# A hybrid decoder layer with expert retrieval: the last mix tile's product in the next phase, y in four parts, two PSUM pairs for the tile sums, 54 candidates

## The chip, the cores and the metric

One core of a Trainium2 chip runs the whole program. The metric is the device time of one execution in microseconds; the kernel before has a median of 3254.82 us over three timed runs (3250.97 to 3257.0). Engines are named as in the profile: TensorE (PE), VectorE (DVE), ScalarE (ACT), GpSimd (POOL) and SyncE (SP), and SP and POOL issue the transfers.

## The reference, cut to what matters

One layer over 1024 prompt rows and 64 sample rows of width 1024, all in float32. Attention and a diagonal state-space mixer work on the same projected input; their outputs are normalised, projected by `w_out` and added to x. Then each row retrieves experts:

```
proj = rmsnorm(x) @ w_in + b_in                      # q, k, v and u
attn = window_attention(q, k, v)                     # window 128, sinks
y    = gelu(Re(C h) + D u);  y = y * sigmoid(y @ w_glu + b_glu)
x    = x + concat(rmsnorm(attn), rmsnorm(y)) @ w_out
xn   = rmsnorm(x)
s    = (xn @ w_query) . keys                         # per head: 2 x 128 scores
top_s, top_i = top_k(s, 16)                          # of either half
best = top_k(top_s[0][:, None] + top_s[1][None, :], 16)   # of 256 pairs
act  = gelu(u_table[idx] . xn)                       # 8 heads x 16 experts
x    = rmsnorm(x + sum(softmax(best) * act * v_table[idx]))
```

Only a pair (a, b) of ranks with (a+1)(b+1) <= 16 can be among the best 16 of the sums, which is why both kernels form far fewer than 256 candidates per head.

## The kernel before, in words

The program has three phases, each a block with a barrier at its end.

**Mix** (`mix_tokens`) walks over eight tiles of 128 prompt rows. In step t it projects tile t+1, computes the attention of tile t and finishes tile t-1: `take_attention` puts the weighted values, scaled, into aT; `mix` multiplies aT by the upper half of `w_out` (w_top) into PJ; `sum_squares` sums sq over the partitions; `mean_square`, `rstd_a` and `add_residual` (L449) make x1 in xk, and `store_x1` writes it to scratch. For the last tile these follow the last step, and the phase ends when SP has seen its stores land. VectorE also makes two matrices for the next phase, in `input_matrices` (L632 to L638): the real one in the last step, the imaginary one after it.

**State-space mixer and sample rows** (`run_ssm_and_samples`). The scan runs on VectorE; TensorE makes the sample attention beside it. At its end TensorE makes the outputs y in four parts (Y_ORDER, four column groups), ScalarE and VectorE copy each from PSUM into U2 and SP stores it as y_ssm. Tile 0's y goes straight to `early.y` by one transfer (L989), issued behind the fourth part.

**Retrieval** (`retrieve_experts`) walks over eight prompt tiles and one of samples. A prompt tile has 128 slots (NSLOT): in each, POOL issues an indirect gather of one row of the joint u and v table per partition, 1 MB, into a ring of eight (L1515). VectorE multiplies the u half by xn and sums it (`product`, L1884). For each pair of slots ScalarE applies GELU (L1637), weighs (L1650) and makes two diagonal matrices (L1657), and TensorE adds the v half times the diagonal into ACC (`add_v`, L2086). Slot s may be gathered again when TensorE is done with it (semaphore pv).

While tile t is gathered, tile t+1 is prepared. `prepared` gives for each slot which step (h, j) of which tile runs there: in steady tiles (t+1, h+1, j) in slot 16h+j, and in the last 16 slots (t+2, 0, j). The steps of row 0 work on y: GELU at (0, 3), turning at (0, 4), its product with w_glu into ZS at (0, 9) (L1969), its sum at (0, 13), sigmoid at (0, 14) (L1574). Row 2 makes the product with the lower half of `w_out` into OP (L1983) and the residual sum xr; rows 3 and 4 the scores (L2008), rows 4 and 5 the best 16 of each half, row 6 the candidates and the best 16 of them, and from (6, 14) on VectorE finds the number of each chosen expert by a subtraction and a reduction over 16 x NCAND columns (L1805, L1806). The candidates share a buffer with yT, their numbers one with z.

Slot 121 (SPREAD) spreads the next tile's rows over two groups: `spread_rows` writes them into OP and TQ (L2065), and `take_rows` copies them to xn (L1631). When a tile ends, VectorE does products 0 and 1 of the next, then `sum_out`: it waits for the last addition, copies ACC (L1890) and sums the squares; `begin` (L2076) on TensorE waits for that copy and opens ACC again with the residual. POOL's `root` stands behind gather 11 (L1542), `norm_out` on VectorE (L1900) behind product 6.

PSUM has eight banks: ACC, TQ, ZS and OP have two each.

## Time and profile before

| what | us |
|---|---|
| median of three runs | 3254.82 (3250.97 to 3257.0) |
| the profiled execution | 3267.73, its span 3265.8 |
| TensorE busy | 2296.5 (70%) |
| VectorE busy | 2172.5 (67%) |
| POOL busy | 1347.3 (41%) |
| ScalarE busy | 931.3 (29%) |
| first gather issued | 442.49 |
| gathers (1088 of them), share of the 16 DMA engines' span | 85.5% |

The profile is of one execution and its times are those of that execution. Its chain of the work that ended last gives 32% of the span to the gathers, 22% to TensorE, 17% to VectorE. The windows used below give for a stretch the busy time of each engine, the mean granted clock of TensorE (1.00 is 2.4 GHz, 0.50 is 1.2 GHz), the share of time in which the DMA engines had packets, and the rate at which they moved them. Many products here run through a line that all tiles share, so a line's mean hides the stage; the stretches don't.

### The profile page before, as it was taken

How to read it: one execution, taken by the hardware profiler on the slowest of the kernel's cores; microseconds unless marked ns; L12 is line 12 of the kernel's file. 1: busy time of each engine (PE TensorE's matmuls, PEld its weight loads, DVE VectorE, ACT ScalarE, POOL GpSimd, SP SyncE). 2: the span in 40 equal slices, each digit the busy share in tenths (PEclk: the TensorE clock that was granted, in tenths of full speed). 3: DMA queues.
4: the chain of work that ended last, by engine and by line, in shares of the span. 5: the costliest groups of instructions: out<-in, count | busy, mean ns of one | idle time of the engine just before them, and what ended most of it. 6: DMA issues, size and time to landing. Idle time of an engine off the chain costs nothing.

```text
span 3265.8 us, 28428 instructions
## 1 busy us (share of the span) xinstructions
PE 2296.5 (70%) x7579; PEld 784.0 (24%) x7579; DVE 2172.5 (67%) x5144; ACT 931.3 (29%) x3193; POOL 1347.3 (41%) x1265
## 2 busy tenths in 40 slices
PE   8998777776685658566856685668566856676576
PEld 4555543311121112111211121112111211121121
DVE  4545568788568656865686568656865686568644
ACT  2222234323222322232223222322232223222222
POOL 1232024444444454444444544444444444444442
PEclk9998898877787788777877887778777878896899
DMA  5223489999999999999999999999999999999998
GB/s 196 79 75 93 119 340 396 365 399 367 421 421 408 416 411 421 406 414 404 421 415 411 420 422 407 408 420 421 409 421 405 421 412 421 404 421 417 421 414 337
DMA packets 187553, 1208.00 MB, mean 370 GB/s; under 512 B 26552, under 2 KB 33768, under 8 KB 46928
## 3 DMA queue, kind: packets, MB, share of 16 engines
q0 software_dynamic: 157344, 1142.99, 85.5%
q1 hardware_dynamic: 30048, 63.20, 5.5%
q8 instruction: 60, 0.98, 0.1%
q14 instruction: 101, 0.83, 0.1%
HBM read 1190.30 MB, written 15.42 MB: 369 GB/s over the span
## 4 chain that ended last, share of the span: by engine, by line
DMA 32%; PE 22%; DVE 17%; issue 7%; ACT 5%; POOL 4%; DVEq 0%; POOLq 0%; ACTq 0%
DMA uv_ring<-in_uv_table,idx 32%; PE ACC L2086 14%; DVE uv_ring L1884 9%; PE ZS L2008 5%; POOL uv_ring L1515 4%; ACT dg L1657 2%; PE OP L1983 1%; ACT dot L1650 1%; DVE idx_f L1806 1%; DVE S L1805 1%; ACT dot L1637 1%; DVE pos L1730 1%; DVE pos L1727 1%; DVE best L1729 0%; DVE yT_and_cand L1728 0%
## 5 line engine op out<-in xcount | busy, mean ns | idle before, releaser
L2086 PE MATMUL ACC<-uv_ring,dg 128*64 128x512 f32 x4352 | 1466.3, 785 | 895.9 <-ACT dg L1657 895.7
L1515 POOL DMA_INDIRECT uv_ring<-in_uv_table,idx x1088 | 1254.5, 1153 | 1546.7 <-PE ACC L2086 1321.6
L1884 DVE CUSTOM_DVE_ANT_0 uv_ring<-uv_ring,xn 128x1024 f32<-128x1024 f32 x1088 | 1325.6, 1226 | 706.1 <-DMA uv_ring<-in_uv_table,idx 667.0
L2086 PEld LDWEIGHTS ACC<-uv_ring,dg 128*64 128x64 f32 x4352 | 341.1, 165 | 1951.0 <-ACT dg L1657 1381.8
L1637 ACT ACTIVATE dot<-dot 128x2 f32<-128x2 f32 x544 | 110.6, 203 | 1886.2 <-DVE dot L1884 1885.9
L1657 ACT ACTIVATE dg<-stack,dot 128x64 f32<-128x64 f32 x1088 | 324.1, 340 | 17.7
L1650 ACT ACTIVATE dot<-gate,dot 128x1 f32<-128x1 f32 x1088 | 261.2, 287 | 18.9
L2008 PE MATMUL ZS<-score_w,xnT 128*128 128x512 f32 x512 | 242.4, 614 | 0.0
L527 PE MATMUL PJ<-w_in,xT 128*128 128x512 f32 (+1 forms) x384 | 143.8, 532 | 3.2 <-DVE pj L407 3.2
L2008 PEld LDWEIGHTS ZS<-score_w,xnT 128*128 128x128 f32 x512 | 93.4, 194 | 158.9 <-issue 158.9
L1884 DVE DVE_READ_ACCUMULATOR2_ANT dot<- 128x1 f32 x1088 | 89.5, 82 | 0.0
L527 PEld LDWEIGHTS PJ<-w_in,xT 128*128 128x128 f32 x384 | 72.8, 193 | 68.7 <-issue 65.8
L1806 DVE TENSOR_REDUCE idx_f<-S 128x16 f32<-128x992 f32 x64 | 75.9, 1186 | 2.2
L1805 DVE TENSOR_TENSOR S<-z_and_cid,pos_f 128x992 f32<-128x992 f32 x64 | 76.1, 1189 | 0.0
L1983 PE MATMUL OP<-w_bot,yT_and_cand 128*128 128x512 f32 x144 | 66.1, 603 | 0.8 <-issue 0.8
L1726 DVE MAX8 top_v<-S 128x8 f32<-128x128 f32 x144 | 41.8, 290 | 25.6 <-ACT S L1589 18.0
L375 ACT ACTIVATE pr<-pr,small_a 128x256 f32<-128x256 f32 x64 | 31.6, 494 | 93.8 <-DVE small_a L470 93.8
L561 PE MATMUL PJ<-w_top,aT 128*128 128x512 f32 x128 | 56.8, 597 | 1.8 <-issue 0.8
L1729 DVE MAX8 top_v<-S 128x8 f32<-128x128 f32 x144 | 42.5, 295 | 15.2 <-DVE S L1728 0.5
L294 POOL TENSOR_SCALAR stat_a<-stat_a 128x1 f32<-128x1 f32 x9 | 1.8, 205 | 104.6 <-ACT xt L360 81.3
L1542 POOL TENSOR_TENSOR stat_e<-stat_e,minus_half 128x1 f32<-128x1 f32 x27 | 17.3, 649 | 66.3 <-DVE stat_e L1761 33.1
L1727 DVE FIND_INDEX8 top_i<-top_v,S 128x8 uint32<-128x128 f32 x144 | 41.1, 285 | 0.6 <-issue 0.6
(337 smaller groups left out, 1598.1 us busy)
## 6 DMA issues: line engine op xcount, KB each, us to landing
uv_ring<-in_uv_table,idx POOLq DMA_INDIRECT x1088, 10.9
score_w<-in_w_query SPq DMA_DIRECT2D x8, 1024.0 KB, 19.2
w_in<-in_w_in SPq DMA_DIRECT2D x8, 640.0 KB, 9.2
xt<-in_x SPq DMA_DIRECT2D x9, 512.0 KB, 4.7
xr<-scratch_x SPq DMA_DIRECT2D x9, 512.0 KB, 8.3
xc<-in_x_columns SPq DMA_DIRECT2D x8, 512.0 KB, 3.9
xk<-in_x SPq DMA_DIRECT2D x8, 512.0 KB, 3.8
scratch_x<-xk SPq DMA_DIRECT2D x8, 512.0 KB, 2.6
```

The costliest lines, as they stand in the source:

```text
L527: ins = nc.tensor.matmul(PJ[:, b, 0:hi - lo], xT[:, j, :], w_in[:, j, lo:hi], start=(j == 0), stop=(j == KD - 1))
L1515: pool.indirect_dma_start(out=ring[:, s_ % RING, :], out_offset=None, in_=a["uv_table"], in_offset=bass.IndirectOffsetOnAxis(ap=idx[:, s_: ...
L1637: A(act_w[:, cols], dot[:, cols], ACT.Gelu).then_inc(gelus, 1)
L1650: ins = A(wgt[:, n:n + 1], gate[:, n:n + 1], ACT.Copy, scale=act_w[:, n:n + 1])
L1657: A(dg[:, s_ % DG, :], stack[:], ACT.Copy, scale=wgt[:, s_:s_ + 1]).then_inc(diags, 1)
L1727: V.max_index(where[:, 0:8], vals[:, 0:8], src)
L1805: dch_(V.tensor_tensor(match, bcast(cid[:, e, :], KS, 1), bcast(pos_f[:, e, :], NCAND, 2), ALU.subtract))
L1806: dch_(V.tensor_reduce(idx_f[:, e, :], match, AX.X, ALU.min, apply_absolute_value=True))
L1884: V.tensor_tensor_reduce(row, row, xn[:, g, :], 1.0, 0.0, ALU.mult, ALU.add, dot[:, s_:s_ + 1]).then_inc(dots, 1)
L1983: ins = nc.tensor.matmul(OP[:, b, :], yT[:, n, :], w_bot[:, n, 512 * b:512 * b + 512], start=(n == 0), stop=(n == SW // P - 1))
L2008: ins = nc.tensor.matmul(ZS[:, bank, :], xnT[:, m, :], score_w[:, c_:c_ + 4, m, :], start=(m == 0), stop=(m == KD - 1))
L2086: ins = nc.tensor.matmul(ACC[GT * g:GT * (g + 1), b, :], dg[:, n % DG, :], ring[:, n % RING, D + 512 * b:D + 512 * b + 512], start=False, ...
```

## The change

1. **Mix.** The last tile's product, its sum of squares and its residual leave the mix phase. aT, sq and the odd x buffer move to `shared`; the next phase's TensorE does the sum of squares and the product right after it has turned the cached keys, into banks 5 to 7; ScalarE copies the sum and, scaled by the root that POOL makes, the product over sq and aT; VectorE adds it to x between the first and the second part of y, and SP stores it behind the second. TensorE's sample outputs wait for ScalarE's copy, since they use the same banks. `input_matrices` moves: the real half ahead of `mean_square` in the last step, the imaginary half into the real one's place.
2. **y.** Each of its four parts is carried to `early.y` by itself, and ScalarE applies GELU to a constant at the end of the second phase.
3. **PSUM.** OP goes; ACC becomes a pair of pairs, used in turns by the tiles. The spreading and the product with `w_out` go into ZS (for the first tile and the second into the pair that is still free). `begin` of the next tile follows `spread_rows`. `sum_out` comes behind product 4 of the next tile, the root behind gather 13, `norm_out` behind product 8. The steps (t+2, 0, j) begin at slot 100 (106 in the first tile) instead of 112.
4. **Candidates.** The blocks of ranks form 54 instead of 62 candidates per head.

The first excerpt is TensorE's order in the second phase: the turning of the cached keys (kc), and what follows it. U2g and XT are the operands of the sample outputs, qT_s the turned queries.

```order
L1244 MATMUL PA<-ident,kc 128x128 x8
L1274 MATMUL PA<-T,qT_s 32x136 x16
L1252 MATMUL PA<-U2g,XT 8x128 x8
L1259 MATMUL PA<-WC_r,H_and_WBt 8x128 x2
L1259 MATMUL PA<-WC_i,H_and_WBt 8x128 x2
```

The same place of the changed kernel:

```order
L1261 MATMUL PA<-ident,kc 128x128 x8
L1266 MATMUL PA<-one_s,sq_and_aT 128x1 x4
L1271 MATMUL PA<-w_top,sq_and_aT 128x512 x8
L1302 MATMUL PA<-T,qT_s 32x136 x16
L1280 MATMUL PA<-U2g,XT 8x128 x8
L1287 MATMUL PA<-WC_r,H_and_WBt 8x128 x2
```

The last mix tile's sum of squares and product now stand between the keys and the scores; they stood at the end of the first phase.

The second excerpt is TensorE's order where one steady tile passes to the next, before the change. The first row is the end of a long run of additions of tile t (four rows to a pair of slots).

```order
L2086 MATMUL ACC<-uv_ring,dg 64x512 x8
L1969 MATMUL ZS<-early,yT_and_cand 128x512 x4
L2065 MATMUL OP<-xn_next,spread 128x512 x2
L2065 MATMUL TQ<-xn_next,spread 128x512 x2
L2086 MATMUL ACC<-uv_ring,dg 64x512 x12
L2076 MATMUL ACC<-xr,ident 128x512 x2
L2086 MATMUL ACC<-uv_ring,dg 64x512 x24
```

And in the changed kernel, where the names of both pairs are printed as ACC:

```order
L1998 MATMUL TQ<-ident,early 128x128 x4
L2128 MATMUL ACC<-uv_ring,dg 64x512 x8
L2009 MATMUL ZS<-early,yT_and_cand 128x512 x4
L2128 MATMUL ACC<-uv_ring,dg 64x512 x24
L2105 MATMUL ZS<-xn_next,spread 128x512 x2
L2105 MATMUL TQ<-xn_next,spread 128x512 x2
L2118 MATMUL ACC<-xr,ident 128x512 x2
L2128 MATMUL ACC<-uv_ring,dg 64x512 x36
```

The residual stood after the tile's last addition and stands now three pairs ahead of it, right behind the spreading; y's product moved away from the spreading by six pairs.

The third is VectorE's order at the same change of tile, before: four products (the last two of tile t, the first two of t+1), then the copy of the sum.

```order
L1756 TENSOR_TENSOR z_and_cid<-ZS,early 128x512
...
L1884 ISA uv_ring,dot<-uv_ring,xn 128x1024
L1884 ISA dot 128x1
L1890 COPY S<-ACC 128x1024
L1892 ISA xn_next,stat_e<-S 128x1024
L1892 ISA stat_e 128x1
L1895 TENSOR_SCALAR stat_e<-stat_e 128x1
L1884 ISA uv_ring,dot<-uv_ring,xn 128x1024
```

In the changed kernel:

```order
L1799 ISA z_and_cid,stat_e<-early 128x512
L1799 ISA stat_e 128x1
L1800 TENSOR_SCALAR stat_e<-stat_e 128x1
L1924 ISA uv_ring,dot<-uv_ring,xn 128x1024
L1924 ISA dot 128x1
L1930 COPY S<-ACC 128x1024
L1932 ISA xn_next,stat_e<-S 128x1024
L1932 ISA stat_e 128x1
```

The copy came before product 2 and comes now behind product 4, and y's own square sum (step (1, 3)) stands ahead of it.

```diff
@@ mix_tokens, VectorE
                         scale_columns(t + 1, 1 - p)
-
+                        if last:
+                            par.input_matrices(nc, dve, 0)
                         mean_square(t - 1)
...
                     if last:
-                        par.input_matrices(nc, dve, 0)
+                        par.input_matrices(nc, dve, 1)
...
                 take_attention(PT - 1)
-                par.input_matrices(nc, dve, 1)
-                mean_square(PT - 1)
-                add_residual(PT - 1, 1)
@@ mix_tokens, TensorE
-                mix(PT - 1)
-                sum_squares(PT - 1)
@@ run_ssm_and_samples, SP
-                    if n == 3:
-                        early.y_in.mark(sp.dma_start(early.y, U2[0:P // L, :].rearrange("c (j n) -> c j n", j=L)))
+                    if n == 2:
+                        sp.wait_ge(ev["x1_7"], 1)
+                        sp.dma_start(s["x1"][bass.ts(PT - 1, P), :], x1_7[:]).then_inc(stores, 16)
                     cols = slice(i * SW // 4, (i + 1) * SW // 4)
+                    sp.dma_start(early.y[:, cols], U2[0:P // L, :].rearrange("c (j n) -> c j n", j=L)[:, :, cols]
+                                 ).then_inc(early.first_y_in, 16)
@@ POOL
+                pool.wait_ge(ev["summed_7"], 1)
+                pool.tensor_scalar(ms_7, ss_7, 1.0 / AW, EPS, ALU.mult, ALU.add).then_inc(ev["ms_7"], 1)
+                pool.wait_ge(ev["ms_7"], 1)
+                pool.tensor_tensor(rstd_7, ms_7, half[:], ALU.pow).then_inc(ev["rstd_7"], 1)
@@ ScalarE
+                act.wait_ge(ev["squares_7"], 1)
+                A(ss_7, XS_7, ACT.Copy).then_inc(ev["summed_7"], 1)
+                act.wait_ge(ev["mixed_7"], 1)
+                act.wait_ge(ev["rstd_7"], 1)
+                A(attention_7, MO_7.rearrange("p b n -> p (b n)"), ACT.Copy, scale=rstd_7).then_inc(ev["scaled_7"], 1)
...
+                act.wait_ge(ev["one"], 1)
+                A(small[:, 7, 0:1], one[:], ACT.Gelu)
@@ VectorE
                 for n, i in enumerate(Y_ORDER):
+                    if n == 1:
+                        dve.wait_ge(ev["scaled_7"], 1)
+                        shared.xk_in.of(dve, PT - 1)
+                        tt(x1_7[:], x1_7[:], attention_7, ALU.add).then_inc(ev["x1_7"], 1)
                     take_outputs(n, i)
@@ TensorE
+                shared.sq_done.of(pe, PT - 1)
+                for r in range(REP):
+                    ins = nc.tensor.matmul(XS_7, shared.sq[:, r, :], one[:], start=(r == 0), stop=(r == REP - 1))
+                ins.then_inc(ev["squares_7"], 1)
+                shared.aT_done.of(pe, PT - 1)
+                for b in range(2):
+                    for r in range(REP):
+                        ins = nc.tensor.matmul(MO_7[:, b, :], shared.aT[:, r, :], w_top[:, r, 512 * b:512 * b + 512],
+                                               start=(r == 0), stop=(r == REP - 1))
+                ins.then_inc(ev["mixed_7"], 1)
...
+                pe.wait_ge(ev["scaled_7"], 1)
                 for i in range(3):
                     sample_outputs(i)
@@ retrieve_experts
-        OUT_AT = LEAD + 3
-        BLOCKS = ((0, 2, 16), (2, 4, 5), (4, 8, 3), (8, 16, 1))
+        SUM_AT, OUT_AT = LEAD + 1, LEAD + 5
+        EARLY_Y = {"first": 106, "steady": 100}
+        BLOCKS = ((0, 1, 16), (1, 2, 8), (2, 4, 5), (4, 8, 3), (8, 16, 1))
...
-                return own + ([(2, 0, j)] if h == EH - 1 else [])
-            if h < EH - 1:
-                return [(t + 1, h + 1, j)]
-            return [(t + 2, 0, j)] if turn == "steady" else []
+            else:
+                own = [(t + 1, h + 1, j)] if h < EH - 1 else []
+            y_step = s_ - EARLY_Y[turn] if turn in EARLY_Y else -1
+            return own + ([(t + 2, 0, y_step)] if 0 <= y_step < KS else [])
+        def spread_bank(t, g):
+            return TQ if g else ACCS[1] if t == 0 else ZS
+        def product_bank(t):
+            return ACCS[1] if t == 1 else ZS
@@ VectorE, retrieve
                         product(t, s_)
+                        if s_ == SUM_AT and turn != "first":
+                            sum_out(t - 1, P, t * NSLOT)
...
-                        for s_ in range(LEAD - 1):
+                        for s_ in range(LEAD):
                             product(t + 1, s_)
-                        sum_out(t, P, t * NSLOT + slots_of(turn))
-                        product(t + 1, LEAD - 1)
@@ TensorE, begin and retrieve
-                    k["acc_taken"].of(pe, t - 1)
+                    k["acc_taken"].of(pe, t - 2)
...
-                    begin(t)
...
                                     k["yT_done"].of(pe, t + 2)
+                                    k["zb_done"].of(pe, t + 2)
+                                k["S_b"].of(pe, t + 1)
                                 for g in range(GROUPS):
                                     spread_rows(t + 1, g)
+                                begin(t + 1)
```

## Rows read from the trace of the kernel before

**Rows 1.** Windows of busy time: us of each engine, clock, DMA share, GB/s.

```profile
core 0: us, PE busy (x) PEld busy (x) DVE busy (x) ACT busy (x) POOL busy (x), PEclk, DMA share, GB/s
450.00:3240.00 2790.00, 1884.72 (x5462) 535.09 (x5463) 1930.91 (x4538) 814.72 (x2884) 1264.32 (x1106) 0.81 1.00 411
450.00:770.00 320.00, 229.41 (x772) 83.72 (x772) 259.14 (x784) 114.57 (x350) 135.57 (x116) 0.81 0.97 387
1175.00:1325.00 150.00, 110.36 (x328) 32.81 (x328) 97.67 (x238) 41.12 (x156) 68.29 (x61) 0.86 1.01 421
775.00:805.00 30.00, 20.76 (x68) 6.56 (x66) 18.71 (x39) 12.63 (x36) 13.57 (x12) 0.84 0.97 376
...
3095.00:3125.00 30.00, 25.17 (x50) 7.19 (x47) 17.42 (x28) 7.62 (x30) 13.99 (x12) 0.83 0.99 398
1030.00:1060.00 30.00, 19.37 (x52) 3.96 (x48) 26.17 (x53) 10.49 (x33) 13.18 (x12) 0.66 0.98 388
...
2990.00:3020.00 30.00, 17.42 (x52) 3.75 (x48) 25.55 (x64) 10.49 (x33) 12.86 (x12) 0.67 1.01 409
```

**Rows 2.** Timeline, end of the mix phase: start, us, engine, line, operation [idle before].

```profile
258.49 0.16 DVE L435 TENSOR_SCALAR stat_a<-X 128x1 f32<-128x1 f32 x1 [5.04 <-PE X L552]
...
269.05 2.19 DVE L440 TENSOR_SCALAR pr<-pr,small_a 128x256 f32<-128x256 f32 x8
271.16 2.29 DVE L632 TENSOR_TENSOR T<-PR_r,BB_r 128x2048 f32<-128x2048 f32 x1
...
274.17 1.91 PE L594 MATMUL SC<-ident,pr 128*128 128x128 f32 x16
...
282.49 0.54 SPq L280 DMA_DIRECT2D scratch_pj<-pj  x1
...
283.21 7.11 PE L561 MATMUL PJ<-w_top,aT 128*128 128x512 f32 x16 [0.83 <-issue]
...
293.69 0.33 SPq L230 DMA_DIRECT2D scratch_x<-xk  x1
296.65 0.33 SPq L957 DMA_DIRECT2D U<-scratch_u  x1
```

**Rows 3.** Timeline of the second phase: TensorE's hole, and a part of y.

```profile
340.44 1.19 PE L1274 MATMUL PA<-T,qT_s 64*32 64x136 f32 x32 [6.66 <-DVE T L1109]
...
341.56 2.94 PE L1252 MATMUL PA<-U2g,XT 128*8 128x128 f32 x16
...
347.51 1.91 PE L1252 MATMUL PA<-U2g,XT 128*8 128x128 f32 x16 [1.16 <-ACT U L1040]
...
383.52 0.69 DVE L1182 COPY U<-PA 128x512 f32<-128x512 f32 x1 [3.20 <-PE PA L1259]
```

**Rows 4.** Timeline of ScalarE at the start of the third phase.

```profile
396.07 1.28 ACT L1568 ACT_TABLE_LOAD   x1 [4.02 <-PEq L2143]
397.36 0.63 ACT L1568 ACTIVATE early<-early 128x512 f32<-128x512 f32 x1
```

**Rows 5.** Timelines of ScalarE, TensorE and VectorE where tile 1 passes to tile 2.

```profile
1130.39 1.28 ACT L1637 ACT_TABLE_LOAD   x1
1130.43 3.68 PE L2086 MATMUL ACC<-uv_ring,dg 128*64 128x512 f32 x8 [5.04 <-ACT dg L1657]
1134.25 1.22 DVE L1890 COPY S<-ACC 128x1024 f32<-128x1024 f32 x1 [2.97 <-PE ACC L2086]
1135.62 3.63 PE L2076 MATMUL ACC<-xr,ident 128*128 128x512 f32 x4 [1.51 <-DVE S L1890]
1148.21 1.28 DVE L1900 SCALAR_TENSOR_TENSOR S<-S,stat_e,g_fin 128x1024 f32<-128x1024 f32 x1 [4.04 <-POOL stat_e L1542]
```

**Rows 6.** TensorE's timeline at slot 121, and the gathers of 1112 to 1166.

```profile
1114.67 3.70 PE L1969 MATMUL ZS<-early,yT_and_cand 128*128 128x512 f32 x8
1118.21 1.88 PE L2065 MATMUL OP<-xn_next,spread 128*128 128x512 f32 x4
...
DMA to landing us min/median/max: 6.7/11.0/15.2
```

**Rows 7.** Groups by form: busy us, mean ns of one, idle before.

```profile
L1805 DVE TENSOR_TENSOR S<-z_and_cid,pos_f 128x992 f32<-128x992 f32 x64 | 76.1, 1189 | 0.0
```

71 lines of the change are left out of this document (40 added, 31 removed).

## The prediction, made before the changed kernel ran

> **What bounds the kernel now.** I read the windows first. From 450 to 3240 us the DMA engines have a busy share of 1.00 [rows 1]: the eight prompt tiles and the sample tile are fetched there, 1088 gathers of 1 MB each. The last column says how far this stage is from its own ceiling. A quiet stretch runs at 421 GB/s, the whole stage at 411 [rows 1]. Against a ceiling of 421.5 the stage loses 2790 x 10.5 / 421.5 = 69.5 us. Nothing can be won there but these microseconds. Where they lie: I took eight stretches of 30 us, each where one tile passes to the next (the first and the last of them are shown); by the same formula they lose 3.2, 3.3, 4.5, 2.4, 2.5, 3.5, 3.6 and 1.7 us, 24.7 in all. Seven stretches, one per tile, in which VectorE chooses the next tile's experts lose 14.1 (2.4 in the first shown, 0.9 in the last). The first tile, 450 to 770, loses 26.2 [rows 1]. That is 65 of the 69.5.
>
> Before 450 us the DMA engines mostly wait, and the time is a chain through the engines: each microsecond taken out of that chain comes off the end, as all gathers come sooner.
>
> The profiled execution took 3267.7 us, 1.9 more than its span, and lies 12.9 above the median of the three timed runs, 3254.8. The sum is made against 3267.7 and then taken off the median; the 0.4% between them changes a saving of 40 us by 0.2.
>
> **Part 1, the end of the mix phase.** Now the last tile's product (16 records, 7.11 us), its sum of squares, the root and the residual stand at the end, and only half of input_matrices runs beside them; the store's issue begins at 293.69 and ends at 294.02, and the next phase starts at 296.65, 2.63 later [rows 2]. Afterwards the last thing that phase waits for is the copy to scratch_pj, issued at 282.49 + 0.54 = 283.03. But one thing gets later first: the first half of input_matrices, three operations of 2.29, 6.8 us from 271.16 with the waits between them, moves ahead of mean_square, into a hole of 5.04 us that ends at 258.49 [rows 2]. It overfills it by about 1.9 us (it can start at 253.4, after scale_columns, and ends at 260.3 instead of 258.5). The second half takes the first's old place, so VectorE stays 1.9 late to the end. TensorE does not: its transposes at 274.17 wait for probabilities that are ready at 269.05 + 2.19 = 271.2 and would be at 273.1 [rows 2]. So the phase ends at 283.03 + 1.9 + 2.63 = 287.6, **-9.1 us**. If the landing of the stores takes a microsecond more or less, -8 to -10.
>
> **Part 2, the product in the next phase.** TensorE has a hole of 6.66 us from 333.78, while VectorE multiplies, until kT is there at 340.44 [rows 3]. The inserted work is 0.95 + 7.11 = 8.1 us at the full clock, so the scores start about 1.4 late, and the sample outputs wait for ScalarE's copy of the product out of PSUM (VectorE takes 1.22 for as many columns [rows 5]) and start at about 343.1 instead of 341.56. Against this, TensorE no longer idles: today the first batch of L1252 after the hole takes 2.94 us, the next 1.91 [rows 3]; with the hole filled I take 1.91 for the first too. Net **+0.5**. The bounds: -0.6 if VectorE's own chain hides it, +1.6 if the batch stays slow, +8 if the product itself ran at the lower clock. What TensorE did before the hole speaks against the last: it was busy without a pause, and the first batch only got slow behind the 6.66 idle. POOL's two small operations on the root lie ahead of the product's end; VectorE's addition of 1024 columns (1.2 us, as its other 1024-column operations) is put between two parts of y, where VectorE waits 3.2 us for each [rows 3], so it is hidden, and so is the store of x1, which goes out two parts before the phase's last store.
>
> **Part 3, y in four parts and the early GELU.** Today y's transfer is issued whole at the end, the next phase starts, ScalarE loads its table for 1.28 us and the GELU starts at 397.36, right behind it [rows 4]. With the table loaded before the phase's end and only a quarter of y left to carry, it can start at 396.1: **-1.3** (0 if the y transfer is what lands last, -2 at best). Here the Trainium skill (ScalarE: Activation LUTs, What ACT_TABLE_LOAD costs) counts a drain of about 1.4 us behind each load, 2.66 in all. The row has the GELU 10 ns behind the load's end, so the drain isn't seen; by the page this term would be -2.7. Fewer candidates on the way to the first gather: -0.1.
>
> **Part 4, the change of tile.** This is the largest term. At the change the chain is: ScalarE loads the sigmoid's table and then GELU's again, the second at 1130.39, between the last two diagonals; the last pair of products starts at 1130.43 at the lower clock (3.68); VectorE, which has stopped for it, copies the sum at 1134.25; only then the residual enters the same PSUM pair at 1135.62 (3.63), and the new tile's first products run at 1139.18. Then VectorE stops again, 4.04 us up to 1148.21, for a root that stands in POOL's queue behind a gather which itself waits for TensorE [rows 5]. Afterwards the new tile has its own pair, its residual is added at step 121 of 128, the sigmoid comes 12 steps earlier (six at the first change), and VectorE takes the sum after product 4, when TensorE has long been done. No wait of this chain is left but the root's: gather 13 must be issued before it, and VectorE wants it after product 8. The order of the two is as now (gather 11, product 6), but nothing has stalled before, so I give it 0 to 2 us, within what the ring hides. I take 85% of 24.7: **-21**. Bounds 0 (the loss stays) and -24.7.
>
> What moves to another place: y's projection (3.70) and the spreading (two halves of 1.88) stood back to back at step 121 at the full clock, 7.4 us [rows 6], and the rate fell only later, at the change itself. Now the projection stands at step 109, and at 121 spreading and residual, 3.8 + 1.9 to 3.6 = 5.7 to 7.4. That is what the ring swallowed before. At the lower clock it would be 7.5 + 3.6 = 11.1, and the projection 7.4.
>
> **Part 5, 54 candidates.** Each of the 64 subtractions and 64 reductions over 992 columns takes 1.19 us [rows 7]; at 864 columns at most 0.15 less each, about 2.2 us of VectorE per tile, and 0.3 on the best-16 searches; one more small operation in each pairwise table gives back about 0.2. In steps 96 to 108 VectorE is full, so the ring refills faster, but the loss of 14.1 begins in the searches before, where only the 0.3 helps. I take **-5** (0 to -14). In the first tile the same pieces shrink: **-3** (0 to -8) of its 26.2; the rest there is TensorE's making of weights, which is not touched.
>
> **The sum.** -9.1 + 0.5 - 1.3 - 0.1 - 21 - 5 - 3 = -39.0. Median 3254.8 - 39 = **3216**.
>
> **Rivals.** *The stall moves (22%).* The residual and the spreading at the lower clock, or the root's wait, cost about 1.3 us per change of tile: part 4 gives 12 instead of 21, the others stay: 3225 to 3238. For it: the granted clock is 0.81 over the stage [rows 1]. Against: 7.4 us were swallowed.
> *VectorE was the cause of more (17%).* With 2.5 us less per tile the ring is never empty, and part 5 gives 14 + 6 instead of 8, part 4 all: 3254.8 - 10 - 24.7 - 20 = 3200.
> *The pairs bring nothing (6%).* The transfers bound the stage, and a late reissue at the change would be paid elsewhere: part 4 is zero, 3254.8 - 18 = 3237, and with part 5 at its lower end 3245. Against: at full rate a lost transfer can't be made up, and the rate never exceeds 421. The Trainium skill (TensorE: Matmul & The Clock Gate, HAM oscillation) reports a transfer-bound matmul kernel in which double-buffering PSUM gave nothing further (126.6 to 125.5 us). There no such stop as that of [rows 5] is described; by its result this rival would hold.
> *The inserted product runs at the lower clock (4%)*: +7.5, 3223.
> *Slower (3%).* One mechanism: between landing and reissue a gather has some slack. Its time to land is 11.0 us in the median and 6.7 at least [rows 6], so about 4.3 us of delay empty the queue. If TensorE is at the lower clock each time, step 109 costs 7.4 - 4.3 = 3.1 and step 121 11.1 - 4.3 = 6.8, 9.9 per tile and 69 in seven: 3216 + 69 = 3285. It decides from 6.5 us per tile on (39 + 6.5, over seven).
>
> **How the numbers follow.** The forecast (3204 to 3227) has 48%, the rivals as above. Eight in ten: from 3199, the good rival, to 3238, where the moved stall ends; what is left out is most of "nothing" and "slower" and the tails. About 0.2%, 6.5 us, is what a measurement of this kernel can tell from no change. Faster by more than that: all but the slower case and a thin tail, 95%; same 2%; slower 3%.
>
> **What would show it.** The second phase starts near 287.6; L1252's first batch takes 1.9; GELU runs without a load ahead; the first gather is issued near 432.4 instead of 442.5; the eight changes of tile run above 415 GB/s and the sum's copy has no wait; the seven choosing stretches rise by 5 to 10 GB/s. I am wrong if the windows around steps 109 to 121 (some 25 to 50 us ahead of the change) fall below 415, or if the first tile takes longer than its 26.2 us of loss allow.

## The result and the profile after

The changed kernel takes 3241.9 us (median of six runs, 3235.5 to 3249.2) beside 3259.9 for the kernel before (six runs, 3251.0 to 3269.8). The ratio is 0.9949, 95% interval 0.9935 to 0.9964, so 12 to 21 us less. A second comparison of the same kernel (after_again, in the table below) gave 0.9958 (0.9945 to 0.9972). There the way to the first gather takes 393.3 us (391.3 in the first profile) and a steady tile loses 4.3 us (4.9): both differences lie in the span that was expected if one profile scatters (4.2 to 4.6, and up to 3). Its time was expected 15 to 20 us less and came 9 to 18 less. Forecast were 39 us less and 3216 us: the sign was right, the size was more than double what came.

The profiled execution took 3244.9 us, 22.9 less than that of the kernel before. Not all of this can be put down to the five parts. Matmul 56 (counted from 0) of the mix phase's first projection stands ahead of all that the parts move, and it starts at 33.32 us instead of 37.16: 3.84 us were there already. Of these, 1.04 stand ahead of matmul 48 (29.81 instead of 30.85), and 2.80 are matmuls of 0.86 us instead of 0.43: from 31 to 34 us TensorE's granted clock is 0.50 (the 1.2 GHz level) in both profiles of the kernel before (before, before_again) and 1.00 in both of the changed one (after, after_again). So this need not be chance of one execution. all_three, with the changed kernel's front, has 0.50 there too and reaches matmul 56 at 37.2; why a program gets the one or the other is open. If the timed runs are as the profiles, up to 3.8 of the 17 us come from here.

I therefore count the way to the first gather from that matmul.

Windows of the kernel after: the eight tiles, then the tile whose first gather is at 1424.5, cut at 60, 120, 220, 270 and 320 us behind it (us, busy us of each engine, granted clock, DMA share, GB/s):

```profile
core 0: us, PE busy (x) PEld busy (x) DVE busy (x) ACT busy (x) POOL busy (x), PEclk, DMA share, GB/s
450.00:3220.00 2770.00, 1876.57 (x5430) 536.00 (x5426) 1898.43 (x4529) 805.54 (x2862) 1251.37 (x1100) 0.82 1.00 412
1424.50:1484.50 60.00, 36.31 (x105) 9.66 (x106) 34.66 (x64) 16.45 (x60) 28.61 (x26) 0.77 1.01 415
1484.50:1544.50 60.00, 43.62 (x132) 13.63 (x128) 32.84 (x54) 15.86 (x61) 27.68 (x24) 0.86 0.99 408
1544.50:1644.50 100.00, 70.93 (x214) 20.43 (x212) 73.39 (x211) 27.07 (x104) 46.68 (x41) 0.88 1.01 421
1644.50:1694.50 50.00, 27.93 (x78) 6.28 (x80) 41.76 (x124) 14.96 (x51) 20.34 (x20) 0.72 1.00 402
1694.50:1744.50 50.00, 32.11 (x96) 8.08 (x92) 36.04 (x60) 16.89 (x55) 23.13 (x20) 0.77 1.02 420
```

The same tile in the kernel before, first gather at 1443.8:

```profile
1443.80:1503.80 60.00, 38.57 (x109) 11.44 (x109) 34.53 (x64) 19.00 (x60) 26.27 (x24) 0.75 0.97 388
1503.80:1563.80 60.00, 43.76 (x125) 12.60 (x122) 33.09 (x53) 16.20 (x62) 28.11 (x24) 0.77 1.01 420
1563.80:1663.80 100.00, 72.51 (x219) 21.22 (x219) 71.72 (x208) 27.37 (x104) 44.83 (x42) 0.88 1.01 421
1663.80:1713.80 50.00, 28.37 (x80) 6.05 (x76) 43.21 (x123) 14.31 (x48) 21.91 (x20) 0.73 1.01 411
1713.80:1763.80 50.00, 30.25 (x83) 6.89 (x84) 38.32 (x62) 13.43 (x53) 24.11 (x20) 0.73 1.01 421
```

This is the case in small. The change of tile, the largest term of the forecast, is mended for the most part: 388 GB/s became 415. But the next 60 us, 420 before, run at 408, and the choosing stretch went from 411 to 402. The whole stage went from 411 [rows 1] to 412.

What the change set out to remove is gone, all the same. Who the copy of the tile's sum and its normalisation waited for, over all nine tiles, in the kernel before (L1890 and L1900), and who waited for y's product there (L1983):

```profile
  PE ACC L2086: 26.6, 9
...
  POOL stat_e L1542: 27.6, 9
...
  DVE xr L1774: 16.6, 4
```

and after (L1930, L1940, and the addition of y's product at step 22, L1814):

```profile
  PE ACC L2128: 5.2, 1
...
  POOL stat_e L1578: 23.1, 9
...
  PE ZS L2023: 20.2, 7
```

The copy waits only once, after the last gather; the eight waits of [rows 5] are gone. The root's wait stayed, 2.6 us each instead of 3.1. The third row is a wait that has grown more frequent: of its 20.2 us 7.3 stand ahead of the first gather, as in the kernel before; the other six are in steady tiles, 1.6 to 3.1 us each and 12.9 in all. The kernel before has this wait in two steady tiles (1.5 and 1.8 us).

**How the tables below are made.** For every tile, from its first gather on, I take the bytes that the packets of the trace moved in a stretch and count as loss the time less bytes / 421.5 GB/s, the formula of the forecast. Shown is the mean of the seven tiles behind the first. "Lateness" is the time from the landing of a row, read as the end of packet 128 (k + 1) of the gathers, to the start of VectorE's product on it, again a mean over seven tiles. The parts are numbered as in the prediction.

| kernel | ratio to before | us less | matmul 56 to first gather | first tile | steady tile | loss 0-60 | 60-120 | 120-220 | 220-270 | 270-320 | sum |
|---|---|---|---|---|---|---|---|---|---|---|---|
| before | 1 | 0 | 405.3 | 348.6 | 327.1 | 2.9 | 0.0 | 0.1 | 2.1 | 0.0 | 5.2 |
| before_again | | | 398.7 | 345.1 | 327.3 | 3.0 | 0.3 | 0.1 | 2.1 | 0.1 | 5.5 |
| front_only | 0.9977 | 7 | 392.1 | 351.2 | 327.0 | 2.5 | 0.5 | 0.2 | 2.0 | 0.0 | 5.1 |
| cand_only | 0.9988 | 4 | 398.6 | 345.5 | 327.4 | 3.1 | 0.4 | 0.3 | 1.7 | 0.0 | 5.6 |
| pairs_only | 0.9973 | 9 | 397.3 | 345.0 | 325.7 | 0.2 | 1.0 | 0.1 | 2.3 | 0.2 | 3.9 |
| after | 0.9949 | 17 | 391.3 | 345.9 | 327.0 | 0.9 | 1.0 | 0.2 | 2.5 | 0.2 | 4.9 |
| after_again | 0.9958 | 14 | 393.3 | 344.5 | 326.5 | 0.7 | 1.2 | 0.2 | 2.1 | 0.2 | 4.3 |
| late_add | 0.9943 | 19 | 388.3 | 344.9 | 326.3 | 0.7 | 0.2 | 0.8 | 2.3 | 0.3 | 4.3 |
| spread_search | 0.9945 | 18 | 391.7 | 346.2 | 326.4 | 0.6 | 1.9 | 0.1 | 0.5 | 1.2 | 4.2 |
| late_norm | 0.9955 | 15 | 390.0 | 347.5 | 327.0 | 0.0 | 0.4 | 0.8 | 3.1 | 0.3 | 4.5 |
| all_three | 0.9928 | 23 | 391.7 | 340.7 | 326.0 | 0.5 | 0.0 | 0.8 | 1.2 | 1.3 | 3.8 |
| all_three_62 | 0.9935 | 21 | 392.9 | 348.0 | 325.7 | 0.5 | 0.0 | 0.5 | 1.2 | 1.6 | 3.9 |
| spread_wide | 0.9934 | 21 | 391.6 | 342.3 | 326.0 | 1.6 | 0.1 | 0.6 | 0.2 | 1.3 | 3.8 |
| light_vector | 0.9891 | 35 | 393.3 | 333.8 | 325.0 | 0.7 | 0.1 | 0.5 | 0.5 | 1.4 | 3.2 |
| light_tensor | 0.9921 | 26 | 391.3 | 340.0 | 325.7 | 0.8 | 0.1 | 0.3 | 1.2 | 1.4 | 3.8 |
| light_both | 0.9899 | 33 | 391.3 | 333.7 | 325.1 | 0.4 | 0.1 | 0.3 | 1.1 | 1.4 | 3.2 |
| bare | 0.9886 | 37 | 391.2 | 334.8 | 324.8 | 0.9 | 0.0 | 0.2 | 1.5 | 0.5 | 3.1 |

The 95% intervals of the ratios are about 0.001 to either side, 3 to 6 us. One profile of one kernel scatters: the sum by 0.3 to 0.5 us per tile, one stretch by up to 0.4, the first tile by 2 to 4 us, the way to the first gather by 6.6 in the kernel before.

### The profile page after: what moved, and what is told of

Its sections match the earlier page's. It is cut to its first block, busy times and chain, and to the rows that moved or that the text cites. A ratio compares the mean times of both kernels' runs of the same rounds, so it can differ in the third digit from the quotient of the medians.

```text
span 3243.1 us, 28469 instructions
## 1 busy us (share of the span) xinstructions
PE 2290.3 (71%) x7579; PEld 785.6 (24%) x7579; DVE 2151.1 (66%) x5174; ACT 932.4 (29%) x3196; POOL 1345.1 (41%) x1266
## 4 chain that ended last, share of the span: by engine, by line
DMA 32%; PE 24%; DVE 17%; issue 7%; ACT 5%; POOL 3%; DVEq 0%; POOLq 0%; ACTq 0%
DMA uv_ring<-in_uv_table,idx 32%; PE ACC L2128 15%; DVE uv_ring L1924 9%; PE ZS L2048 6%; POOL uv_ring L1551 3%; ACT dg L1696 2%; PE ZS L2023 1%; ACT dot L1689 1%; PE ZS L2009 1%; ACT dot L1676 1%; DVE idx_f L1846 1%; DVE S L1845 1%; DVE pos L1769 1%; DVE pos L1766 1%; PE ZS L2079 0%
## 5 line engine op out<-in xcount | busy, mean ns | idle before, releaser
L1846 DVE TENSOR_REDUCE idx_f<-S 128x16 f32<-128x864 f32 x64 | 67.4, 1053 | 2.2
L1845 DVE TENSOR_TENSOR S<-z_and_cid,pos_f 128x864 f32<-128x864 f32 x64 | 67.4, 1054 | 0.0
L2023 PE MATMUL ZS<-w_bot,yT_and_cand 128*128 128x512 f32 x128 | 62.3, 633 | 0.8 <-issue 0.8
L555 PE MATMUL PJ<-w_top,sq_and_aT 128*128 128x512 f32 x112 | 49.7, 597 | 1.0
```

What stands on the lines that cost most here:

```text
L1845: dch_(V.tensor_tensor(match, bcast(cid[:, e, :], KS, 1), bcast(pos_f[:, e, :], NCAND, 2), ALU.subtract))
L1846: dch_(V.tensor_reduce(idx_f[:, e, :], match, AX.X, ALU.min, apply_absolute_value=True))
L2023: ins = nc.tensor.matmul(product_bank(t)[:, b, :], yT[:, n, :], w_bot[:, n, 512 * b:512 * b + 512], start=(n == 0), stop=(n == SW // P - 1))
```

## The experiments

**1. front_only: the parts ahead of the gathers alone.** The kernel before with the edits of parts 1 to 3 and the stage of the eight tiles unchanged.

> The kernel before with parts 1, 2 and 3 of the change alone (mix end, last product in the next phase's hole, y in four parts with the early GELU); the eight tiles' stage is that of before. Theory A (the gain of the change lies ahead of the first gather): the first gather is issued 14 us earlier than in the kernel before (17.8 in the profiled pair, of which 3.84 were already there at the 56th matmul of the first projection, so not the change's), the tiles lose as before, 5.2 us each in the steady ones; time 14 us less, about 3246 where the kernel before has 3260 (10 to 17 less). Rival B (the retrieval gave its share too and the profiled pair only hides it): 10 us less, as predicted for these parts, and the other 8 come from parts 4 and 5. Of the 14, 3.6 us stand where the landing of BU is waited for; if that was luck of one run, this run shows about 10.

Measured: ratio 0.9977 (0.9968 to 0.9986), 7 us less. Theory A's 14 is refuted, B's 10 lies just within the interval. The profile tells why: the first gather comes 392.1 us behind matmul 56, 13 less than in the first profile of the kernel before, but that profile was slow there (next run). Matmul 56 itself starts 3.2 us earlier than in the kernel before, so a part of the 7 us may stand ahead of the edits.

**2. before_again: a second profile of the kernel before.**

> The kernel before, profiled once more. Of the 17.8 us by which the first gather came earlier in the profiled pair, 3.84 stood already behind the 56th matmul of the first projection. In cand_only, whose code ahead of the gathers is this kernel's, the rest takes 398.6 us instead of 405.3. If the first profile was slow there by chance, this one gives about 399 and the true gain of parts 1 to 3 is 8 us; if cand_only was the lucky one, about 405 and 14. A steady tile should lose 5.2 us again, within 0.4.

Measured: 398.7, as cand_only (398.6); a steady tile loses 5.5 us, within the 0.4. Of the 6.6 us between the two profiles of one program 3.5 lie in one wait, TensorE's timeline of the second phase, kernel before, first profile:

```profile
311.29 3.71 PE L1216 MATMUL PA<-ident,U2g 128*128 128x128 f32 x32
318.49 2.64 PE L1222 MATMUL PA<-ident,BU 8*128 8x8 f32 x32 [3.49 <-DMA BU<-scratch_u]
```

and before_again:

```profile
309.76 3.71 PE L1216 MATMUL PA<-ident,U2g 128*128 128x128 f32 x32
313.41 2.14 PE L1222 MATMUL PA<-ident,BU 8*128 8x8 f32 x32
```

BU landed late once; another 1.6 us lie ahead of it in the phase and 1.3 behind it. So parts 1 to 3 are worth 398.7 - 391.3 = 7.4 us, which front_only's time (5 to 10 us) agrees with. My expectation A had taken the luck of one profile for a gain.

**3. cand_only: 54 candidates alone.**

```
-        BLOCKS = ((0, 2, 16), (2, 4, 5), (4, 8, 3), (8, 16, 1))
+        BLOCKS = ((0, 1, 16), (1, 2, 8), (2, 4, 5), (4, 8, 3), (8, 16, 1))
```

> The kernel before with 54 candidates instead of 62 and nothing else. Theory A: VectorE falls behind in the nine steps 81 to 89, where each step is 2.82 us long for a row every 2.49 and only 0.04 us of each are saved, while step 81 pays 0.17 more for the fifth block; so the choosing stretch (220 to 260 us behind a tile's first gather) still loses about 2.1 us per tile, only the first tile gains 2 to 3: time 0 to 4 us less. Rival B (what I predicted, the 2.2 us saved per tile in steps 94 to 108 fill the ring): choosing stretch down to 1.2 us or less per tile, time 8 us less.

Measured: 0.9988 (0.9979 to 0.9997), 1 to 7 us less, and the steady tiles are no shorter (327.4). Theory A holds and B's 8 us are refuted. That the saving stands in the first tile this profile can't show: 345.5 us lie between the 348.6 and the 345.1 of the two profiles of the kernel before. all_three_62 points there further down.

**4. pairs_only: the two PSUM pairs alone.** All edits of part 4 in the kernel before.

> The kernel before with part 4 alone: two PSUM pairs in turns, residual and spreading at step 121, sum taken at step 4 and normalised at 8, y's projection at step 109; 62 candidates, front as before. Theory C (one reserve): the stretch of 0 to 60 us behind a tile's first gather loses 1 us instead of 2.9, but 60 to 120 us loses about 1 instead of 0 and the rest does not fall, a steady tile loses 4.6 to 5.2 (5.2 before), time 1 to 5 less. Rival D (what I predicted): 3 us less per tile, 21 in all.

Measured: 0.9973 (0.9963 to 0.9983), 9 us less, a steady tile loses 3.9 instead of 5.2 to 5.5. That is more than C's 1 to 5 us and less than half of D's 21; the tile's sum, too, is below C's 4.6 to 5.2. Both are refuted in their numbers. The 60 us behind the change of tile lose 0.2 instead of 2.9 to 3.0, then 1.0 come up at 60 to 120 us. So of the 2.8 us that the stretch gave back the tile kept about half, 1.3 to 1.6.

**5. late_add: without the new wait.**

```
-                    elif at == (2, 6):
+                    elif at == (2, 8):
```

on VectorE and for the root on POOL, and the scaling at (2, 13) instead of (2, 12). The place in the kernel after, TensorE, VectorE and POOL at step 22 of the tile that begins at 1751.7:

```profile
1820.82 3.70 PE L2023 MATMUL ZS<-w_bot,yT_and_cand 128*128 128x512 f32 x8
...
1824.56 0.69 DVE L1814 TENSOR_TENSOR xr<-ZS,xr 128x512 f32<-128x512 f32 x1 [2.95 <-PE ZS L2023]
...
1828.40 1.99 POOL L1551 DMA_INDIRECT uv_ring<-in_uv_table,idx  x1 [0.30 <-issue]
1834.07 1.55 POOL L1551 DMA_INDIRECT uv_ring<-in_uv_table,idx  x1 [3.68 <-PE ACC L2128]
```

VectorE stops for 2.95 us, its products come late, TensorE's after them, and POOL issues one gather at 1828.40 and the next 5.7 us later, at 1834.07. At 1835.5 only five packets are under way.

> The changed kernel with VectorE's addition of the projection to the residual two steps later (step 24 instead of 22, the root of it on POOL as well, the scaling at 29 instead of 28). In the changed kernel VectorE waits 1.6 to 3.1 us for that product at step 22 and the rate falls 80 to 100 us behind the tile's first gather, 1.1 us lost per tile (7.5 in seven; the kernel before loses nothing there). Theory A (the wait is the cause): the wait is gone and with it the loss at 80 to 100 us; 5 to 8 us less than the changed kernel, some 24 less than the kernel before. Rival B (the loss is due to the 16 DMA engines being apart, which the old stall at the change of tile used to reset, and any disturbance will do): the loss appears elsewhere, total of a steady tile stays at 4.9 us, the time at 18 less than the kernel before.

Measured: the wait is gone, and so is the loss of that stretch (1.0 to 0.2). But 120 to 220 us rose from 0.2 to 0.8, the sum is 4.3, as after_again has it, and the time, 0.9943 (0.9929 to 0.9956), can't be told from the changed kernel's. For the stretch A was right. The time speaks for B, but its interval doesn't exclude the lower end of A's 5 to 8 us. In the last of the seven tiles 2.3 us went between 110 and 150 us behind its first gather, where at first VectorE waits for nothing but the transfers.

**6. spread_search: VectorE's worst stretch thinned out.** In the changed kernel steps 82 to 89 last 2.8 us each for a row every 2.49, and VectorE's lateness grows to 6.5 us.

```
+        SEARCH_AT = (2, 3, 5, 6, 8, 9, 11, 12)
...
-                    elif h == 6 and 2 <= j < 2 + EH:
-                        e = j - 2
+                    elif h == 6 and j in SEARCH_AT:
+                        e = SEARCH_AT.index(j)
```

> The changed kernel with the eight searches for the best 16 of the candidates at steps 82, 83, 85, 86, 88, 89, 91, 92 instead of 82 to 89 in a row, and what follows them three steps later (93 instead of 90, ScalarE's exponentials at 95 instead of 92). Theory A (VectorE's lateness, 6.5 us behind the landing at step 90 in the mean, makes the loss of 2.6 us per tile at 220 to 260 us): lateness stays below 4 us, that loss falls under 0.8 per tile, 10 to 14 us less than the changed kernel, about 30 less than the kernel before. Rival B (TensorE's products of the next weights or POOL's gathers bound that stretch): the loss stays at 2.6 per tile and the time within 3 us of the changed kernel, 18 less than before.

Measured: lateness at most 4.5 us behind step 66, and the loss of 220 to 270 us falls from 2.5 to 0.5, as A says. But 60 to 120 us lose 1.9 (1.0), the last 50 us 1.2 (0.2). Sum 4.2, time 0.9945 (0.9931 to 0.9958): nothing that can be told from the changed kernel, and not A's 10 to 14 us. A's cause was right and its gain did not come.

**7. late_norm: without the root's wait.**

```
-        SUM_AT, OUT_AT = LEAD + 1, LEAD + 5
+        SUM_AT, OUT_AT = LEAD + 1, LEAD + 8
```

> The changed kernel with the normalisation of the output at step 11 instead of 8 and nothing else. At step 8 VectorE waits 2.5 us for the root; at 11 it should not. Theory C (one reserve): the first 30 us behind a tile's first gather lose 0.5 instead of 0.9 us, VectorE's lateness at step 9 falls from 4.5 to about 2, and the tile's sum stays within 0.4 us of the changed kernel's; time within 3 us of it. Rival D: the whole 0.9 us per tile are saved, 6 us less than the changed kernel.

Measured: L1940 now waits 0.7 us in all instead of 23.1:

```profile
  POOL stat_e L1578: 0.7, 1
```

The first 60 us lose nothing (0.9 before), lateness at step 9 is 2.3 instead of 4.5, and 120 to 270 us lose 1.1 us more. Sum 4.5, time 0.9955 (0.9942 to 0.9968). Theory C; D's 6 us less did not come.

**8. all_three: the three edits together.**

> The changed kernel with three disturbances taken away at once: the residual's addition at step 24 (as in late_add), the searches of the candidates spread out (as in spread_search), and the output's normalisation at step 11 instead of 8, where VectorE waits 2.5 us for a root. Loss of a steady tile so far: before 5.2 us, changed 4.9, late_add 4.3, spread_search 4.2, though the stretch that each of the two mends lost 0.8 and 2.0 us less: the rest came up elsewhere. Theory C (one common reserve, drawn down by whatever stretch comes next, and by the 16 DMA engines being apart, which a stall resets): again a steady tile loses 3.5 us or more, in TensorE's score stretch (90 to 150 us) and after 230 us; time 18 to 24 less than the kernel before. Rival D (the losses are separate): 0.2 + 0.3 + 0.5 + 0.7, about 2 us per tile, time 35 to 40 less than the kernel before.

Measured: 0.9928 (0.9915 to 0.9941), 3234.5 us, and 3.8 us lost per tile. C holds (3.5 or more, 18 to 24 us); D, which added up the stretches, is refuted. It has the lowest time of the kernels here that leave nothing out, about 8 us below the changed one, though the intervals of all_three_62 and spread_wide overlap with its own; by its one profile some 5 of the 8 are in the first tile (340.7), which scatters by 2 to 4.

**9. all_three_62: the same with 62 candidates.**

> all_three with 62 candidates again. Theory E (the candidates save in the first tile alone): first tile 3 us longer than all_three's 340.7, steady tiles as all_three (3.8 us lost each), time 3 us more: 20 less than the kernel before. Rival F (the fifth block at step 81 takes back in the steady tiles what it saves in the first): steady tiles lose 3.0 to 3.4 each and the time is within 1 us of all_three.

Measured: 0.9935 (0.9922 to 0.9948); first tile 7 us longer, steady tiles the same (3.9 and 3.8). That is theory E's picture, the candidates worth something in the first tile alone, and F's 3.0 to 3.4 us per tile are refuted. The times of the two kernels can't be told apart, and of the 7 us, where E expected 3, 2 to 4 can be scatter.

**10. light_vector, light_tensor, light_both: take the compute away.** In light_vector a search is

```
+                def best8(vals, where, src):
+                    dch_(V.max(vals[:, 0:8], src), True)
+                    dch_(V.max_index(where[:, 0:8], vals[:, 0:8], src), True)
+                    V.tensor_copy(vals[:, 8:16], vals[:, 0:8])
+                    dch_(V.tensor_copy(where[:, 8:16], where[:, 0:8]), True)
```

and in light_tensor

```
-                        for m in range(2 * part, 2 * part + 2):
+                        for m in range(2 * part, 2 * part + 1):
```

> all_three, and in the steady steps each search for the best 16 finds 8 and writes them twice (of five operations MATCH_REPLACE8, the second MAX8 and the second FIND_INDEX8 are left out, two small copies come in), so the experts chosen are not the reference's; all transfers stay. Theory C1 (VectorE draws the reserve down): VectorE's lateness at steps 64 to 108 stays under 3 us and a steady tile loses under 1.5. Theory C2 (TensorE's score stretch, or the DMA engines' own spread, takes what VectorE leaves): it loses 3 us or more, as all_three.

> all_three, and of the 32 score products of a tile's steps 35 to 55 every second one is left out (half of the sum over the 1024 columns, so other experts are chosen than the reference's); transfers stay. C1 (VectorE): loss of a tile as all_three. C2a (TensorE, whose score steps make a pair of rows last 5.5 us for 4.97 of transfer where the clock is low): loss of the stretch from 80 to 150 us falls to zero and a steady tile loses 1.5 us less. C2b (DMA engines' spread alone): no difference to all_three beyond 0.5 us per tile.

> all_three with both left out, half of each steady search and half of the score products. If the compute engines make the losses (C1, C2a), a steady tile loses under 1 us and a tile takes 323 us (321.9 with no loss). If the transfer has a loss of its own (C2b), it stays at 3 us or more and the tile at 325.

These kernels choose other experts than the reference; what they fetch is as much. Measured: less VectorE takes 0.6 us off a tile's loss (3.8 to 3.2), far from C1's 1.5 (the lateness at steps 64 to 108 still reached 4.6 us, where C1 asked for under 3), and 7 us off the first tile (333.8), more than half of its 12. Less TensorE takes 0.5 from the score stretch (0.8 to 0.3), which comes back elsewhere; sum 3.8, C2b. Both together: 3.2 again, and a tile of 325.1 us, as expected if the transfer has a loss of its own. Taking work from the compute engines no longer moves the steady tiles much.

**11. spread_wide: all of VectorE's choosing under its full load.**

```
-        EARLY_Y = {"first": 106, "steady": 100}
+        EARLY_Y = {"first": 106, "steady": 107}
...
+        SEARCH_AT, MATCH_AT = range(98, 114, 2), range(114, 138, 3)
```

> The changed kernel with the later addition and the later normalisation of all_three, and VectorE's choosing spread over steps 82 to 120 at under its full load: searches at every second step 82 to 96, the scaled numbers at 97, the matches at every third step 98 to 119, sums and picks at 120; the early part of y at 107 instead of 100, since it shares a buffer with the numbers. all_three still loses 2.4 us per tile between 220 us and the tile's end, where VectorE is 3 to 4.6 us behind the landing. Theory C1 (that lateness is what draws the reserve down): it stays near the landing's own 2.5 us there, that loss falls to about 1 per tile, a steady tile loses 2.5 us, time 8 to 10 less than all_three, 31 to 34 less than the kernel before. Rival C2 (what VectorE leaves is taken by the spread of the DMA engines): the loss is within 0.5 us of all_three's 3.8 and the time within 3 us.

Measured: 220 to 270 us lose 0.2, the rest of the tile 1.3, and the change of tile 1.6 again; sum 3.8, ratio 0.9934 (0.9921 to 0.9948). C2: within 0.1 us per tile of all_three. VectorE's lateness stayed at 3.1 to 4.5 us there and not near the 2.5 that C1 asked for, so C1's mechanism was not put to a full test.

**12. bare: almost nothing left of the choosing.** light_both, and

```
+                        if e > 0:
+                            return
```

ahead of the matches.

> light_both (half of every steady search and half of the score products left out) and seven of the eight matches left out too, so stale but valid numbers of earlier rows are fetched and the experts are not the reference's; the transfers are as many. light_both still loses 3.2 us per tile, 2.4 of them behind 220 us, where the matches stand. If VectorE's load there is the cause, a steady tile now loses under 1.2 us and lasts 323; if the transfers lose by themselves, it stays at 2.5 or more.

Measured: 3.1 us per tile and 324.8 for its length, where under 1.2 and 323 were expected if VectorE's load were the cause and 2.5 or more if the transfers lose by themselves. Windows of bare, the whole stage and the choosing stretch of the tile that begins at 1410.7:

```profile
450.00:3220.00 2770.00, 1764.13 (x5200) 480.40 (x5200) 1689.66 (x3858) 809.82 (x2881) 1264.00 (x1102) 0.83 1.00 413
...
1630.70:1680.70 50.00, 28.55 (x80) 6.13 (x80) 34.00 (x95) 15.01 (x52) 22.76 (x20) 0.73 1.00 409
```

and of all_three:

```profile
450.00:3220.00 2770.00, 1862.63 (x5443) 529.90 (x5444) 1907.14 (x4541) 809.38 (x2877) 1267.04 (x1102) 0.83 1.01 413
```

217 us less work on VectorE (1907.14 to 1689.66), 99 less on TensorE, and the rate, in whole GB/s, is 413 in both. Here VectorE waits for the transfers at every row, by its timeline in that stretch:

```profile
1653.22 1.23 DVE L1934 CUSTOM_DVE_ANT_0 uv_ring<-uv_ring,xn 128x1024 f32<-128x1024 f32 x1 [1.25 <-DMA uv_ring<-in_uv_table,idx]
...
1661.75 1.23 DVE L1934 CUSTOM_DVE_ANT_0 uv_ring<-uv_ring,xn 128x1024 f32<-128x1024 f32 x1 [1.77 <-DMA uv_ring<-in_uv_table,idx]
```

## Why the prediction was wrong, point by point

**Part 1, -9.1: right.** From matmul 56 to the first row of the second phase it takes 259.5 us in the four profiles of kernels with the old end and 250.0 to 251.5 in the thirteen with the new: -9.0 in the mean. Timeline of the kernel after, where [rows 2] had the store at 293.69 and the phase at 296.65:

```profile
281.23 0.52 SPq L279 DMA_DIRECT2D scratch_pj<-pj  x1
284.16 0.33 SPq L956 DMA_DIRECT2D U<-scratch_u  x1
```

The start named, 287.6, was missed by 3.4 only because this execution was 3.84 ahead at matmul 56.

**Part 2, +0.5: nearly.** The inserted product runs at the full clock and the first batch behind it too; ScalarE's copy sits between them as foreseen (kernel after, answering [rows 3]):

```profile
315.66 7.11 PE L1271 MATMUL PA<-w_top,sq_and_aT 128*128 128x512 f32 x16
...
322.70 0.72 PE L1302 MATMUL PA<-T,qT_s 64*32 64x136 f32 x32
322.81 1.11 ACT L1055 ACTIVATE sq_and_aT<-PA,stat 128x1024 f32<-128x1024 f32 x1 [6.80 <-PE PA L1271]
324.07 1.91 PE L1280 MATMUL PA<-U2g,XT 128*8 128x128 f32 x16 [0.65 <-ACT sq_and_aT L1055]
```

From BU's transposes to the scores it is 20.7 us in before_again and cand_only (22.0 in the slow first profile, 19.0 in pairs_only) and 21.7 in most of the changed ones: +1.0, inside the bounds.

**Part 3, -1.4: right, a little under.** From those scores to the GELU it went from 56.8 to 54.9, -1.9; the load stands in the old phase now (kernel after, answering [rows 4]):

```profile
373.56 1.28 ACT L1078 ACT_TABLE_LOAD   x1
374.86 0.20 ACT L1078 ACTIVATE small_s<-one_s 128x1 f32<-128x1 f32 x1
...
377.60 0.63 ACT L1607 ACTIVATE early<-early 128x512 f32<-128x512 f32 x1 [2.54 <-PEq L2188]
```

Again the activation stands 20 ns behind the load's end, as in [rows 4]; the drain of about 1.4 us that the Trainium skill (ScalarE: Activation LUTs, What ACT_TABLE_LOAD costs) counts behind a load is not seen in this trace either. Of the parts ahead of the gathers 10.0 were forecast and 7.4 came. The difference is what I had not priced: from the GELU to y's product 0.7 us more, from there to the first gather 0 to 2.9 more, and up to BU's transposes 0.7 more in the mean (15.9 to 19.6 us in thirteen profiles with the new front, 16.7 to 17.6 in three with the old, the slow first one left aside). Why these grew no run shows; loads that don't start earlier with the chain would fit.

**Part 4, -21: the step that failed.** The term took 85% of the losses of eight windows as won once the waits were gone. The waits went as described. Answering [rows 5] and [rows 6], VectorE's copy at a change of tile and TensorE's step 121:

```profile
1119.94 1.22 DVE L1930 COPY S<-ACC 128x1024 f32<-128x1024 f32 x1
...
1133.11 1.28 DVE L1940 SCALAR_TENSOR_TENSOR S<-S,stat_e,g_fin 128x1024 f32<-128x1024 f32 x1 [2.73 <-POOL stat_e L1578]
```

```profile
1097.30 3.15 PE L2105 MATMUL ZS<-xn_next,spread 128*128 128x512 f32 x4
1100.29 1.88 PE L2105 MATMUL TQ<-xn_next,spread 128*128 128x512 f32 x4
1102.01 1.88 PE L2118 MATMUL ACC<-xr,ident 128*128 128x512 f32 x4
```

6.9 us at step 121, inside the 5.7 to 7.4 given, and the ring does swallow them: the last 50 us of a tile lose 0.2. What was wrong is that the window's loss was taken for the price of the stop in it. Instead of 21 us the pairs alone are worth 9, 5 to 12 by the interval (pairs_only); in the changed kernel a steady tile loses 0.7 us less than before in the mean of two profiles each, about 5 in seven and 2 to 8 with the scatter. The loss came up again behind the change of tile, at the wait for y's product, which the working had not looked at: it costs the changed kernel 1.0 to 1.2 us per tile between 60 and 120 us, and late_add, which has no such wait, 0.2. The three pieces measured alone, 7 (parts 1 to 3), 9 and 4, add up to 20 and the whole came to 14 to 17, the same within their intervals; so the forecast of 39 was too large in each of them, most in this one. I had taken the root's wait at "0 to 2 us, within what the ring hides", and it was 2.6; late_norm shows that taking it away brings nothing that can be measured either.

**Part 5, -8: mis-sized.** The row of [rows 7] became

```profile
L1845 DVE TENSOR_TENSOR S<-z_and_cid,pos_f 128x864 f32<-128x864 f32 x64 | 67.4, 1054 | 0.0
```

135 ns less each, near the 0.15 at most. The whole part is worth 1 to 7 us (cand_only) instead of 8, which leaves room for the 3 of the first tile. The 5 in the steady tiles did not come, cand_only's last 327.4 us: the loss begins in the searches ahead, as the text said, and it should have set the term to zero on that ground. The 0.2 us that the fifth block was to take back did not come either: step 81, which makes all pairwise sums, takes 3.84 us instead of 3.83, and the eight searches behind it save 0.3 in all.

**The rivals.** The 3242 lie near "the pairs bring nothing" (6%), between its 3237 and 3245. Its mechanism, a late reissue that "would be paid elsewhere", is half of what the runs found: the pairs did bring 9 us, and the number fits because other terms fell short too. "The stall moves" (22%) was right that it moves and wrong where: steps 109 and 121 cost nothing, step 22 did. Its argument against, that 7.4 us were swallowed, held for its own place and said nothing about the next. The 24.7 us were to be had only if every stretch stood for itself.

**What bounds the stage.** Eight rows are in the ring. A landed row is used by VectorE and TensorE and then asked for again; what is left of the eight, about four (11.0 us from issue to landing, a row every 2.49), is the reserve of the 16 DMA engines. My reading is that each disturbance draws it down. In the kernel before the change of tile cost most, 2.9 us. Behind it VectorE's lateness was as low as 1.4 us at steps 16 to 22 (1.8 in before_again), and the same wait for y's product (1.9 us at step 22 in the tile shown) cost nothing. In the changed kernel the lateness there is 2.0, in late_add 2.2, in bare 2.5, although VectorE stands idle between its rows. The trace has the end of each gather itself, and there VectorE starts 0.02 us behind it. So lateness with an idle VectorE is the transfers' own: when row k is complete, 101 packets of the following rows (of 128 to a row) have landed already in the changed kernel, 70 in the kernel before, 124 in bare. Not all of the lateness is such a spread, as the very last gather, with nothing behind it, also ends 0.45 us behind its last packet. The Trainium skill (DMA: Bandwidth & Descriptors, Why a DMA increments its semaphore by 16 and not by 1) says that a DMA's engines finish independently and that only the full 16 means that all data has landed; the trace agrees with it as far as these numbers go.

The rate does not wait for the whole reserve to be empty. In the changed kernel 1.2% of the packets take over 0.4 us instead of 0.311, and what they take beyond that adds up to 4.3 us per engine and tile, beside a loss of 4.9 per tile. Three quarters of this time lie in packets that start while 128 or more packets, a whole row's worth, are still to start of gathers issued at least 2.2 us before (the gather issued at 1834.07 us above moved its first packets at 1836.3). Single engines that have run out while others have work would look like this.

So two things are shown. The losses of the stretches are not independent: late_add, spread_search, late_norm, all_three and spread_wide each freed one or more of them and kept 3.8 to 4.5 us of a sum of 4.3 to 4.9. And the work of VectorE and TensorE is not what makes the larger part of the rest: with 217 us of VectorE's and 99 of TensorE's gone a tile still loses 3.1 us of 322. That the engines' drifting apart is its cause, and that the old stall set it back, was only argued. For it: the landing lags the count of packets by 2.5 us in the last eight steps of a tile in both kernels, and in steps 8 to 15 of the next by 1.2 to 1.6 in the kernel before (two profiles), by 2.1 in the changed one. Against it: from the kernel before to bare this lag grows, 1.9 to 2.9 us in the mean, while the loss falls. The trace doesn't tell the 16 engines apart, and no run changed what each of them carries. An untested rival is the way from a landing to the reissue of its slot through VectorE, ScalarE, TensorE and POOL: it takes 8.4 to 9.1 of the ring's 19.9 us even in bare, and no run changed the number of slots. The cause of the last 3.1 us stays open.

## What to carry to other kernels

In a stage that the transfers of a ring bound, don't add up the losses of stretches: they share one ring, and a stretch that runs at full rate today may lose when an earlier stall is gone (here 420 to 408 GB/s). Before a stall is priced, ask which wait comes next with less reserve (here 2 us at step 22), and ablate the suspected work first: one run with the work left out (bare) gives an idea of what re-ordering that work can win, here about 2 us per tile of the 5 that the windows show. And compare two profiles of the same program before a difference of a few microseconds between two programs is explained: here 3.5 us at one landing were chance, while 3.8 at the start came again in both profiles of each program.

## What the runs showed of the hardware that I had not expected

- A restart after a nearly empty queue is dear. A packet of 8192 bytes takes 0.311 us in the median; when the ring refilled at 1836.3 us in the kernel after, 18 packets started within 0.4 us and eleven of them took 0.53 to 1.14.
- The DMA share says little about the rate: at a share of 1.00 to 1.01 the windows above have 402, 409 and 421 GB/s. The packets are longer where the rate is low: between 220 and 270 us of the changed kernel's tiles the mean gather packet takes 0.326 us, between 120 and 220 us 0.315.
- A row's completion came 2.0 us (after) to 2.9 us (bare, mean of the seven tiles) behind the landing of as many packets as it has, for whole stretches of 50 us and more, with VectorE waiting.
- The same program, profiled twice, waited 3.49 us for one landing (BU) in one execution and not at all in the other.
